# One attention and mixture-of-experts layer: rotary keys, latent query products and the second S5 turn set in another order

## The chip, the core and the metric

One core of a Trainium2 chip runs the whole program. The metric is device time in microseconds: 941.87 us, the median of 3 runs of the kernel before (941.67 to 942.17). In the profile PE is TensorE's matmul row and PEld its weight loads, DVE is VectorE, ACT ScalarE, POOL GpSimd, and SP the engine that issues most DMAs. Everything is computed in float32.

## What is computed

One layer for 512 latent tokens and 256 context tokens, width 1024. All tokens are normalised and modulated, and go through one input projection. Its columns feed three groups of heads:

```
z_lat = split_in_proj(modulate(rms_norm(x, norm_mix_g), sh_m, sc_m) @ w_in)    # u | q | k | v | cq | ckv | kr
z_ctx = split_in_proj(modulate(rms_norm(ctx, norm_mix_g), csh_m, csc_m) @ w_in)
s5  : h[t] = lam_bar * h[t-1] + b_bar @ u[t], forwards and backwards; y = Re(c_mat @ h) + d * u
      y = gelu(y);  y = y * sigmoid(y @ w_glu + b_glu)
diff: softmax(q0 k0') - lam * softmax(q1 k1'), times v; q and k of latent tokens are rotated
mla : q = rms_norm(cq) @ w_uq;  k_nope, v = rms_norm(ckv) @ w_ukv;  the 32 rotary columns kr are shared by all heads
x = x + g_m * (concat(s5, diff, mla) @ w_out)
x = rms_norm(x + g_f * moe(modulate(rms_norm(x, norm_ffn_g), sh_f, sc_f)))     # 32 experts, two per token
```

The modulation vectors (sh, sc, g) are silu(c) times a 1024 x 6144 matrix.

## The kernel before

Tokens stand in six tiles of 128: tiles 0 and 1 are context, 2 to 5 latent. Each engine has its program written out by hand, one list of steps per engine, and the steps meet at semaphores. An engine takes its own steps in the written order; nothing is planned at run time ahead of the experts. The list of TensorE (L941 to L1006) is the one that the change rewrites, with those of ScalarE (L1560 to L1611) and VectorE (L2174 to L2236).

The steps that matter here:

- `project(kind, t)` multiplies tile t with the columns of one kind: q, k, v are 512 wide, m (the latent columns cq, ckv, kr) 416 wide for a latent tile and 160 for context. Each is eight products over the model width. `project("uq", t)` is the latent query product, 2 products of 384 columns, from the turned cq of tile t. The result lands in one of four PSUM banks in turn; `z_bank` waits until the tile four places earlier in the list `ztiles` has been copied out (`z_free`).
- `evacuate(w)` on VectorE copies such a result out, rotated where it must be, into one of two buffers (QR). For v tiles `v_out` on ScalarE does it, or VectorE for v5 in the kernel before.
- `turn_tile(w)` transposes the copied tile on TensorE, into bank 4 or 5 by turns; `turn_out(w)` on ScalarE copies it to its place. The list `turns` numbers them: a turn waits for the turned tile two places earlier to be out.
- `turn_rope` transposes the rotary keys of all six tiles at once, into banks 4 and 5; ScalarE makes four copies of it (L1526), one per head.
- The S5 group: `s5_turn(d)` turns the input matrices of direction d, in four pieces c of four transposes, into banks 6 and 7, and ScalarE copies them out (`s5_evac_turned`, L1545). Pieces 2 and 3 wait for the copies of pieces 0 and 1. `s5_inputs(d, r)` multiplies them with u, VectorE's `s5_scan(d)` copies the results (L2059), runs the recurrence (L2083), and sets the flag `hh` (L2094) that `s5_outputs(d)` on TensorE waits for. The outputs of direction 1 also need taps (TPL) that POOL fetches after the last input product (L584 to L588). `s5_add` on VectorE (L2104) adds the outputs up.
- `mod_sum(g, r)` on VectorE adds up two of eight slices of a third of the modulation product from a 2 MB piece of w_mod; the piece's slot is free for the next load when it is done. `summed_rows` on TensorE sums them over partitions.
- `gated` is the S5 gate's product; `scores(u)` begins attention.

VectorE's list has m0, m1, m2, the scan of direction 1, m3, two modulation sums, `s5_add(1)`, m4, and so on. Around the scan it is the same in both kernels.

At the end, from about 440 us on, the experts run in blocks, and their weights (1 MB and 2 MB pieces) stream through the slots that the front has given back. Their loads are issued by SP, the first of them after all projected tiles are made and out, after attention, and after the output projection.

Of the kernel before, what the change touches and what calls it, by code (L numbers as in the profile page):

```python
# [75 lines left out]
def build(nc, a, out):  # L76
# [22 lines left out]
    with ctx:  # L99
# [219 lines left out]
        U_BANK = (0, 1, 6, 7, 0, 1)  # L319
        ztiles = [("u", n) for n in range(NU)]  # L320
        ztiles += [("q", t) for t in range(NCT, NT)] + [("k", t) for t in range(NT)] + [("m", t) for t in range(NT)]
        ztiles += [("v", t) for t in range(5)] + [("uq", 2), ("uq", 3), ("uq", 4), ("v", 5), ("g", 0), ("g", 1), ("uq", 5)]
        ztiles += [("kn", i) for i in range(4)] + [("nv", i) for i in range(3)]
        zi = {w: n for n, w in enumerate(ztiles)}
        turns = [w for w in ztiles if w[0] in ("q", "k", "m")] + [("uq", 2), ("uq", 3), ("kr", 0), ("uq", 4), ("uq", 5)]
        ti = {w: n for n, w in enumerate(turns)}
        ACT_TILES = (("nv", 0), ("nv", 1))

# [357 lines left out]
        def _(pe):  # L686
# [189 lines left out]
                                     start=(r == 0), stop=(r == 1))  # L876
                ins.then_inc(sem("kk"), 1)

            def s5_turn(d):
                pe.wait_ge(sem("pb"), d + 1)  # L880
                for c in range(4):
                    if c == 0:
                        pe.wait_ge(sem("ksb"), 2 * d + 1)
                    elif c >= 2:
                        pe.wait_ge(sem("pbt"), 4 * d + c - 1)
                    for j in range(4):
                        r, q = divmod(4 * c + j, NPAIR)
                        ins = tr(bank(6 + c % 2, P, j * P), PB[:, r, q].rearrange("p i n -> p (i n)"), ident)
                    ins.then_inc(sem("pb_t"), 1)
# [77 lines left out]
            project("m", 1)  # L967
            project("m", 2)
            turn_tile(("k", 5))
            s5_turn(1)  # L970
            turn_tile(("m", 0))
            s5_inputs(1, 0)
            turn_tile(("m", 1))
            s5_inputs(1, 1)
            project("m", 3)
            project("m", 4)
            project("m", 5)
            project("v", 0)
            turn_tile(("m", 2))
# [4 lines left out]
            pe.wait_ge(sem("yacc"), 4)  # L984
            project("v", 2)
            turn_tile(("m", 4))
            project("v", 3)
            turn_tile(("m", 5))
            summed_rows(1, 6, True)
            project("v", 4)  # L990
            project("uq", 2)
            project("uq", 3)
            project("uq", 4)
            project("v", 5)
            turn_tile(("uq", 2))
            turn_tile(("uq", 3))
            gated()
            turn_rope()
            project("uq", 5)
            turn_tile(("uq", 4))  # L1000
            summed_rows(2, 7, False)
            mod_rows(2, KD // 2 - 1, 7)
            turn_mod(1, 6)
            project_latent("kn", 0)
            project_latent("kn", 1)
            turn_tile(("uq", 5))  # L1006

            def scores(u):

# [407 lines left out]
        def _(act):  # L1417
# [121 lines left out]
                else:  # L1539
                    A(ksb[:, :, 0:7 * GRP], taps[:, :, 0:7 * GRP], ACT.Copy).then_inc(sem("ksb"), 1)  # L1540

            def s5_evac_turned(d):
                for c in range(4):
                    act.wait_ge(sem("pb_t"), 4 * d + c + 1)
                    A(PBT[:, c // 2, 4 * (c % 2):4 * (c % 2) + 4].rearrange("p q s -> p (q s)"), bank(6 + c % 2), ACT.Copy).then_inc(  # L1545
                        sem("pbt"), 1)
# [27 lines left out]
            squares_of_m(1)  # L1574
            squares_of_m(2)
            turn_out(("k", 5))
            s5_evac_turned(1)

            act.wait_ge(sem("k_out"), 16)
            turn_out(("m", 0))  # L1580
            turn_out(("m", 1))
            squares_of_m(3)
            squares_of_m(4)
            squares_of_m(5)
            def v_out(t):
                act.wait_ge(sem("z"), zi[("v", t)] + 1)
                act.wait_ge(sem("z_free"), zi[("v", t)])
                A(VV[:, t, :], bank(zi[("v", t)] % 4), ACT.Copy).then_inc(sem("z_free"), 1)

            turn_out(("m", 2))  # L1590
            turn_out(("m", 3))
            v_out(0)
# [1 line left out]
            turn_out(("m", 4))  # L1594
            v_out(2)
            turn_out(("m", 5))
            v_out(3)
            act.wait_ge(sem("gelu_in"), 1)
            A(yt1, yt1, ACT.Tanh, scale=math.sqrt(2.0 / math.pi)).then_inc(sem("tanh"), 1)
            v_out(4)  # L1600

            turn_out(("uq", 2))
            turn_out(("uq", 3))
            for mo in range(2):
                act.wait_ge(sem("z"), zi[("g", mo)] + 1)
                A(yt1[:, mo].rearrange("p j c -> p (j c)"), bank(zi[("g", mo)] % 4), ACT.Sigmoid,
                  bias=cols[:, R_BGLU + mo:R_BGLU + mo + 1]).then_inc(sem("s5_sig"), 1)
            turn_out(("kr", 0))
            mod_copy(1, 6)
            turn_out(("uq", 4))  # L1610
            turn_out(("uq", 5))  # L1611


# [168 lines left out]
        def _(dve):  # L1782
# [340 lines left out]
            def evacuate(w):  # L2123
                kind, t = w
                dve.wait_ge(sem("z"), zi[w] + 1)
                src = bank(zi[w] % 4)
                n = ti.get(w)
                if n is not None:
                    if n >= 2:
                        dve.wait_ge(sem("turned"), n - 1)  # L2130
                    dst = QR[:, n % 2, :]
                lt = t - NCT
                if kind in ("q", "k"):
                    if t >= NCT:
                        rope(dst.rearrange("p (h f) -> p h f", h=2 * DH), src.rearrange("p (h f) -> p h f", h=2 * DH),
                             2 * DH, DHD // 2, lt, 0)
                    else:
                        st(cp(dst, src))
                elif kind == "v":
                    st(cp(VV[:, t, :], src))  # L2140
                elif kind == "m":
                    dve.wait_ge(sem("m_ms"), t + 1)
                    if t >= NCT:
                        st(V.reciprocal(sml[:, 16 + t:17 + t], sml[:, 16 + t:17 + t]))
                    st(V.reciprocal(sml[:, 24 + t:25 + t], sml[:, 24 + t:25 + t]))
                    st.settle()
                    if t >= NCT:
                        st(ts(dst[:, 0:QRANK], src[:, 0:QRANK], sml[:, 16 + t:17 + t], None, ALU.mult))
                    st(ts(dst[:, QRANK:QRANK + KVRANK], src[:, QRANK:QRANK + KVRANK], sml[:, 24 + t:25 + t], None, ALU.mult))
                    kr = src[:, QRANK + KVRANK:QRANK + KVRANK + MR]  # L2150
                    if t >= NCT:
                        rope(KR[:, t:t + 1, :], kr.unsqueeze(1), 1, MR // 2, lt, 32)
                    else:
                        st(cp(KR[:, t, :], kr))
                elif kind == "uq":
                    s3 = src[:, 0:MH * MQ].rearrange("p (h f) -> p h f", h=MH)
                    d3 = dst[:, 0:MH * MQ].rearrange("p (h f) -> p h f", h=MH)
                    st(cp(d3[:, :, 0:MN], s3[:, :, 0:MN]))
                    rope(d3[:, :, MN:], s3[:, :, MN:], MH, MR // 2, lt, 32)
                elif kind == "kn":  # L2160
                    pr, half = divmod(t, 2)
                    t0, nt = (0, 512) if half == 0 else (512, TOK - 512)
                    for g in range(2):
                        st(cp(MKT[0:MN, 2 * pr + g, t0:t0 + nt], src[MN * g:MN * (g + 1), 0:nt]))
                else:
                    st(cp(MVV[:, 2 * t:2 * t + 2, :].rearrange("p t e -> p (t e)"), src))
                st.settle()
                if n is not None:
                    cp(sml[:, 506:507], epsb[:, :]).then_inc(sem("qr"), 1)
                if w == ("uq", 2):  # L2170
                    dve.wait_ge(sem("z_free"), zi[w])
                cp(sml[:, 507:508], epsb[:, :]).then_inc(sem("z_free"), 1)

# [20 lines left out]
            evacuate(("m", 4))  # L2194
            mod_sum(1, 2)
            evacuate(("m", 5))
            mod_sum(1, 3)
            dve.wait_ge(sem("y_in"), 32)
            for h in range(2):
                st(stt(YT[:, h], UT[:, h, :, NCC:], cols[:, R_SD + h:R_SD + h + 1], YT[:, h], ALU.mult, ALU.add))  # L2200
# [8 lines left out]
            st(ts(yt1, yt1, 0.5, 0.5, ALU.mult, ALU.add))  # L2209
            st.settle()  # L2210
            tt(YG, yt1, YT, ALU.mult).then_inc(sem("yg"), 1)
            mod_sum(2, 1)
            evacuate(("uq", 2))
            evacuate(("uq", 3))
            cp(sml[:, 511:512], epsb[:, :]).then_inc(sem("qr"), 1)
            mod_sum(2, 2)
            evacuate(("uq", 4))
            evacuate(("v", 5))
            dve.wait_ge(sem("yg"), 1)
            for mo in range(2):  # L2220
                dve.wait_ge(sem("s5_sig"), mo + 1)
                tt(mix[:, mo, :].rearrange("p (c j) -> p j c", j=CH), YG[:, mo], yt1[:, mo], ALU.mult).then_inc(
                    sem("s5_mix"), 1)
                cp(sml[:, 509 + mo:510 + mo], epsb[:, :]).then_inc(sem("z_free"), 1)
            evacuate(("uq", 5))
            mod_cols(1, (4, 4), 6, "modc")
            def maxima(u):
                dve.wait_ge(sem("scores"), u + 1)
# [523 lines left out]
```

## Time and profile before

| | |
|---|---|
| median of 3 runs | 941.87 us (941.67 to 942.17) |
| profiled execution | 944.54 us, its span 942.8 us |
| TensorE busy | 854.7 us, 91% of the span |
| VectorE, ScalarE busy | 451.1 us, 246.6 us |
| granted TensorE clock, mean | 0.975 |
| chain that ended last | PE 44%, issue 39%, POOL 5%, DVE 4%, DMA 3%, ACT 2% |

The chain is followed back from the last instruction to what released each step; "issue" is time in which an engine waited for nothing that the profile shows. A row of a timeline has the start in us, the busy time, the engine, the line and operation, what it writes and reads, how many instructions are merged, and in brackets the idle time before it and what ended that. Float32 products show as several records each, so 16 records of L854 are one tile of 8 products. The granted clock is 1.00 or 0.50 of full speed (2.4 or 1.2 GHz); a value between is a mean over the stretch.

### The profile page before, as it was taken

How to read it: one execution, taken by the hardware profiler on the slowest of the kernel's cores; microseconds unless marked ns; L12 is line 12 of the kernel's file. 1: busy time of each engine (PE TensorE's matmuls, PEld its weight loads, DVE VectorE, ACT ScalarE, POOL GpSimd, SP SyncE). 2: the span in 40 equal slices, each digit the busy share in tenths (PEclk: the TensorE clock that was granted, in tenths of full speed). 3: DMA queues.
4: the chain of work that ended last, by engine and by line, in shares of the span. 5: the costliest groups of instructions: out<-in, count | busy, mean ns of one | idle time of the engine just before them, and what ended most of it. 6: DMA issues, size and time to landing. Idle time of an engine off the chain costs nothing.

```text
span 942.8 us, 12686 instructions
## 1 busy us (share of the span) xinstructions
PE 854.7 (91%) x4395; PEld 431.5 (46%) x4395; DVE 451.1 (48%) x1112; ACT 246.6 (26%) x561; POOL 138.5 (15%) x376
## 2 busy tenths in 40 slices
PE   4999999999899999999999999999999976867786
PEld 1765546554445556446344444444444432333232
DVE  4596888978688674125652221312222321212127
ACT  4701023213467654022211120211111211111113
POOL 1411001020010010000012121212212222212110
PEclk9999999999999999999899999999999999788999
DMA  9961204586400391225989999999999999999985
GB/s 372 343 190 32 89 1 120 153 343 225 152 2 23 111 321 60 89 112 217 376 341 381 420 419 420 419 421 420 421 421 419 419 418 419 418 417 421 418 349 223
DMA packets 56373, 267.12 MB, mean 283 GB/s; under 512 B 10867, under 2 KB 17325, under 8 KB 29456
## 3 DMA queue, kind: packets, MB, share of 16 engines
q1 hardware_dynamic: 44416, 249.70, 65.9%
q0 software_dynamic: 11712, 16.86, 6.4%
q8 instruction: 23, 0.38, 0.2%
q14 instruction: 14, 0.11, 0.0%
q10 hardware_dynamic: 208, 0.06, 0.0%
HBM read 264.48 MB, written 25.17 MB: 307 GB/s over the span
## 4 chain that ended last, share of the span: by engine, by line
PE 44%; issue 39%; POOL 5%; DVE 4%; DMA 3%; ACT 2%; POOLq 1%; SPq 1%; DVEq 0%
PE PS L854 15%; PE PS L1089 6%; PE PS L1020 4%; POOL held L650 2%; PE PS L1027 2%; PE PS L1058 2%; DMA S5Z<-in_w_mod 2%; PE PS L778 2%; POOL BIG L659 2%; DMA BIG<-pair_d 1%; PE PS L1067 1%; PE PS L1218 1%; PE PS L924 1%; PE PS L1247 1%; PE PS L1319 1%
## 5 line engine op out<-in xcount | busy, mean ns | idle before, releaser
L854 PE MATMUL PS<-BIG 128*128 128x512 f32 (+2 forms) x352 | 139.6, 553 | 0.0
L854 PEld LDWEIGHTS PS<-BIG 128*128 128x128 f32 x352 | 64.2, 190 | 66.7 <-issue 66.1
L1322 PE MATMUL PS<-S5Z,QKV 128*128 128x512 f32 x192 | 83.4, 592 | 0.0
L1347 PE MATMUL PS<-BIG,GM 128*64 128x512 f32 x320 | 75.4, 614 | 4.0 <-DMA BIG<-in_moe_w 4.0
L650 POOL TENSOR_TENSOR held<-held 1x1 f32<-1x1 f32 x141 | 25.8, 183 | 302.2 <-PE PS L1295 178.4
L2670 DVE TENSOR_TENSOR QKV<-PS,QKV 64x512 f32<-64x512 f32 x48 | 33.0, 688 | 68.4 <-PE PS L1347 46.2
L1311 PE MATMUL PS<-BIG,QKV 128*32 128x256 f32 x768 | 49.5, 409 | 17.5 <-DMA BIG<-in_moe_w 17.5
L1319 PE MATMUL PS<-BIG,QKV 128*64 128x512 f32 x256 | 57.1, 596 | 3.9 <-DMA BIG<-in_moe_w 3.9
L1089 PE MATMUL PS<-BIG 128*128 128x512 f32 x128 | 57.0, 596 | 0.0
L1322 PEld LDWEIGHTS PS<-S5Z,QKV 128*128 128x128 f32 x192 | 36.1, 190 | 43.0 <-issue 43.0
L1720 ACT ACTIVATE QKV<-PS,fcp 128x128 f32<-128x128 f32 x120 | 45.1, 456 | 34.9 <-PE PS L1295 34.9
L2596 DVE TENSOR_SCALAR QKV<-PS,fcp 128x128 f32<-128x128 f32 x120 | 40.9, 403 | 21.6 <-PE PS L1295 21.6
L2229 DVE TENSOR_REDUCE sml<-PS 128x1 f32<-128x768 f32 x48 | 44.8, 952 | 12.8 <-PE PS L1020 12.6
L1295 PE MATMUL PS<-CST,BIG 128*128 128x128 f32 x240 | 37.2, 302 | 13.0 <-DMA BIG<-xh_d,gidx 13.0
L1731 ACT ACTIVATE wglu<-PS 128x256 f32<-128x256 f32 (+1 forms) x16 | 7.4, 464 | 156.6 <-PE PS L1322 80.1
L1295 PEld LDWEIGHTS PS<-CST,BIG 128*128 128x128 f32 x240 | 31.9, 196 | 31.7 <-DMA BIG<-xh_d,gidx 17.6
L1619 ACT ACTIVATE BIG<-PS,sml 128x768 f32<-128x768 f32 x48 | 43.1, 897 | 8.8 <-DVE sml L2229 8.4
L1352 PE MATMUL PS<-S5Z,GM 128*128 128x512 f32 x96 | 43.9, 612 | 0.0
L2602 DVE TENSOR_TENSOR GM<-wglu,PS 64x256 f32<-64x256 f32 x15 | 6.4, 425 | 74.8 <-ACT wglu L1728 74.8
L1311 PEld LDWEIGHTS PS<-BIG,QKV 128*32 128x32 f32 x768 | 24.6, 116 | 37.4 <-DMA BIG<-in_moe_w 20.7
L1347 PEld LDWEIGHTS PS<-BIG,GM 128*64 128x64 f32 x320 | 22.0, 141 | 42.9 <-issue 41.4
L2606 DVE TENSOR_TENSOR GM<-wglu,PS 128x512 f32<-128x512 f32 x6 | 4.1, 688 | 78.4 <-ACT wglu L1731 78.4
(576 smaller groups left out, 1239.3 us busy)
## 6 DMA issues: line engine op xcount, KB each, us to landing
BIG<-in_moe_w SPq DMA_DIRECT2D x84, 1024.0 KB, 22.5
BIG<-in_moe_w SPq DMA_DIRECT2D x21, 2048.0 KB, 25.7
S5Z<-in_moe_w SPq DMA_DIRECT2D x40, 1024.0 KB, 20.7
BIG<-in_w_mod SPq DMA_DIRECT2D x11, 2048.0 KB, 7.7
S5Z<-in_moe_w SPq DMA_DIRECT2D x10, 2048.0 KB, 24.3
BIG<-in_w_in SPq DMA_DIRECT2D x3, 2048.0 KB, 18.7
QKV<-in_x SPq DMA_DIRECT2D x8, 512.0 KB, 8.8
BIG<-in_w_out SPq DMA_DIRECT2D x2, 2048.0 KB, 10.9
```

Of the source, the lines that this page charges most:

```text
L650: pool.tensor_tensor(held[:, cell:cell + 1], held[:, 0:1], held[:, 0:1], ALU.add)
L854: ins = mm(dst[:, c0:width], hT[:, k, tok], wslot(n, width)[:, k, c0:width], start=(k == 0), stop=(k == KD - 1))
L1089: ins = mm(bank(op_bank(i)), mix[:, k, t * P:(t + 1) * P], wslot(n)[:, k, :], start=(k == 0), stop=(k == KD - 1))
L1295: ins = tr(bank(k // 4, P, (k % 4) * P), hg.rearrange("p (q k) -> p k q", k=KD)[:, k, :], ident)
L1311: ins = mm(PS[32 * n:32 * n + 32, 1024:1280], few, w13(side)[:, w, k, 256 * m:256 * m + 256], start=(k == 0), stop=(k == KD - 1))
L1319: ins = mm(PS[r, 1024:1536].rearrange("p (m h) -> p m h", m=2), few, w13(side)[:, :, k, 256 * m:256 * m + 256], start=(k == 0), stop=(k == ...
L1322: ins = mm(bank(2 + m), hgT[:, k, :], w13(side)[:, m, k, :], start=(k == 0), stop=(k == KD - 1))
L1347: ins = mm(PS[64 * n:64 * n + 64, 2560:3072], hidT[:, k % 2, 64 * (k // 2):64 * (k // 2) + 64], w2s(side)[:, k, 512 * n:512 * (n + 1)], st ...
L1352: ins = mm(bank(5 + n), hidT[:, k, :], w2s(side)[:, k, 512 * n:512 * (n + 1)], start=(k == 0), stop=(k == 3))
L1619: A(pbuf[:, 2 * (b % 2) + m, :], unit_row(u), ACT.Exp, bias=sml[:, 64 + u:65 + u], accum_out=sml[:, 160 + u:161 + u]).then_inc(sem("probs" ...
L1720: ins = A(hgT[:, k, :], bank(0, P, k * P), ACT.Identity, scale=fcp[:, 0, k:k + 1], bias=fcp[:, 1, k:k + 1])
L2229: V.tensor_reduce(sml[:, 64 + u:65 + u], unit_row(u), AX.X, ALU.max, negate=True).then_inc(sem("nmax"), 1)
```

## The change

TensorE's list is reordered in two places, and the lists of ScalarE and VectorE follow.

1. The turn of S5's direction 1 is cut in two halves. Pieces 0 and 1 come behind k5's turn as before. Then m0's turn and the product of latent row tile m3 stand ahead of pieces 2 and 3, and m1's turn and the product of m4 stand ahead of both input groups. Before, both input groups came ahead of m3.
2. The rotary keys are turned behind m5's turn and the product uq3, ahead of the summed rows. Before, they came behind the gate's product. The latent query products uq2 to uq5, before three in a row between v4 and v5 and one behind the rotary turn, are spread between the v tiles. v5 goes to ScalarE. VectorE copies uq2 and uq3 ahead of the GELU's input, uq4 and uq5 behind it. No instruction on data is added or left out.

The diff, cut to its core:

```diff
         ztiles = [("u", n) for n in range(NU)]
         ztiles += [("q", t) for t in range(NCT, NT)] + [("k", t) for t in range(NT)] + [("m", t) for t in range(NT)]
-        ztiles += [("v", t) for t in range(5)] + [("uq", 2), ("uq", 3), ("uq", 4), ("v", 5), ("g", 0), ("g", 1), ("uq", 5)]
+        ztiles += [("v", 0), ("v", 1), ("v", 2), ("uq", 2), ("uq", 3), ("v", 3), ("uq", 4), ("v", 4), ("uq", 5), ("v", 5)]
+        ztiles += [("g", 0), ("g", 1)]
         ztiles += [("kn", i) for i in range(4)] + [("nv", i) for i in range(3)]
         zi = {w: n for n, w in enumerate(ztiles)}
-        turns = [w for w in ztiles if w[0] in ("q", "k", "m")] + [("uq", 2), ("uq", 3), ("kr", 0), ("uq", 4), ("uq", 5)]
+        turns = [w for w in ztiles if w[0] in ("q", "k", "m")] + [("kr", 0)] + [("uq", t) for t in range(NCT, NT)]
         ti = {w: n for n, w in enumerate(turns)}
...
@@ -967,13 +968,14 @@
             project("m", 1)
             project("m", 2)
             turn_tile(("k", 5))
-            s5_turn(1)
+            s5_turn(1, (0, 1))
             turn_tile(("m", 0))
+            project("m", 3)
+            s5_turn(1, (2, 3))
+            turn_tile(("m", 1))
+            project("m", 4)
             s5_inputs(1, 0)
-            turn_tile(("m", 1))
             s5_inputs(1, 1)
-            project("m", 3)
-            project("m", 4)
             project("m", 5)
             project("v", 0)
             turn_tile(("m", 2))
@@ -984,26 +986,26 @@
             pe.wait_ge(sem("yacc"), 4)
             project("v", 2)
             turn_tile(("m", 4))
+            project("uq", 2)
+            turn_tile(("m", 5))
+            project("uq", 3)
+            turn_rope()
+            summed_rows(1, 6, True)
             project("v", 3)
-            turn_tile(("m", 5))
-            summed_rows(1, 6, True)
+            turn_tile(("uq", 2))
+            project("uq", 4)
             project("v", 4)
-            project("uq", 2)
-            project("uq", 3)
-            project("uq", 4)
+            turn_tile(("uq", 3))
+            project("uq", 5)
             project("v", 5)
-            turn_tile(("uq", 2))
-            turn_tile(("uq", 3))
+            turn_tile(("uq", 4))
             gated()
-            turn_rope()
-            project("uq", 5)
-            turn_tile(("uq", 4))
+            turn_tile(("uq", 5))
             summed_rows(2, 7, False)
             mod_rows(2, KD // 2 - 1, 7)
             turn_mod(1, 6)
             project_latent("kn", 0)
             project_latent("kn", 1)
-            turn_tile(("uq", 5))
...
@@ -1574,19 +1576,20 @@
             squares_of_m(1)
             squares_of_m(2)
             turn_out(("k", 5))
-            s5_evac_turned(1)
-
-            act.wait_ge(sem("k_out"), 16)
-            turn_out(("m", 0))
-            turn_out(("m", 1))
-            squares_of_m(3)
-            squares_of_m(4)
-            squares_of_m(5)
+            s5_evac_turned(1, (0, 1))
+
...
+            act.wait_ge(sem("k_out"), 16)
+            turn_out(("m", 0))
+            s5_evac_turned(1, (2, 3))
+            squares_of_m(3)
+            turn_out(("m", 1))
+            squares_of_m(4)
+            squares_of_m(5)
             turn_out(("m", 2))
             turn_out(("m", 3))
             v_out(0)
@@ -1594,20 +1597,20 @@
             turn_out(("m", 4))
             v_out(2)
             turn_out(("m", 5))
-            v_out(3)
+            turn_out(("kr", 0))
             act.wait_ge(sem("gelu_in"), 1)
             A(yt1, yt1, ACT.Tanh, scale=math.sqrt(2.0 / math.pi)).then_inc(sem("tanh"), 1)
+            v_out(3)
+            turn_out(("uq", 2))
+            mod_copy(1, 6)
             v_out(4)
-
-            turn_out(("uq", 2))
             turn_out(("uq", 3))
+            v_out(5)
+            turn_out(("uq", 4))
...
-            turn_out(("kr", 0))
-            mod_copy(1, 6)
-            turn_out(("uq", 4))
             turn_out(("uq", 5))
...
@@ -2194,7 +2197,10 @@
             evacuate(("m", 4))
             mod_sum(1, 2)
             evacuate(("m", 5))
+            cp(sml[:, 511:512], epsb[:, :]).then_inc(sem("qr"), 1)
             mod_sum(1, 3)
+            evacuate(("uq", 2))
+            evacuate(("uq", 3))
...
             tt(YG, yt1, YT, ALU.mult).then_inc(sem("yg"), 1)
+            evacuate(("uq", 4))
             mod_sum(2, 1)
-            evacuate(("uq", 2))
-            evacuate(("uq", 3))
-            cp(sml[:, 511:512], epsb[:, :]).then_inc(sem("qr"), 1)
+            evacuate(("uq", 5))
             mod_sum(2, 2)
-            evacuate(("uq", 4))
-            evacuate(("v", 5))
```

TensorE around the second S5 turn, before. L888 are the turns of the input matrices, L815 the turns of m0 and m1, L903 the input products, L854 with 128x416 the latent row tiles, with 128x512 v0, L917 the first of the outputs:

```order
L888 MATMUL PS<-CST,BIG 128x128 x16
L815 MATMUL PS<-CST,S5Z 128x128
L903 MATMUL PS<-S5Z 64x96 x16
L815 MATMUL PS<-CST,S5Z 128x128
L903 MATMUL PS<-S5Z 64x96 x16
L854 MATMUL PS<-BIG 128x416 x24
L854 MATMUL PS<-BIG 128x512 x8
L815 MATMUL PS<-CST,S5Z 128x128 x3
L917 MATMUL PS<-S5Z 128x64 x16
```

and in the changed kernel, where all lines behind the lists stand one number higher:

```order
L889 MATMUL PS<-CST,BIG 128x128 x8
L816 MATMUL PS<-CST,S5Z 128x128
L855 MATMUL PS<-BIG 128x416 x8
L889 MATMUL PS<-CST,BIG 128x128 x8
L816 MATMUL PS<-CST,S5Z 128x128
L855 MATMUL PS<-BIG 128x416 x8
L904 MATMUL PS<-S5Z 64x96 x32
L855 MATMUL PS<-BIG 128x416 x8
L855 MATMUL PS<-BIG 128x512 x8
L816 MATMUL PS<-CST,S5Z 128x128 x3
L918 MATMUL PS<-S5Z 128x64 x16
```

One latent tile has moved ahead of the second half turn, one more ahead of the input products, which stand together now.

TensorE around the rotary keys, before. L716 are the summed rows, L860 the latent query products, L818 their turns, L937 the gate, L827 the turn of the rotary keys:

```order
L716 MATMUL PS<-BIG,CST 32x512 x4
L854 MATMUL PS<-BIG 128x512 x8
L860 MATMUL PS<-wuq,S5Z 128x384 x6
L854 MATMUL PS<-BIG 128x512 x8
L818 MATMUL PS<-CST,S5Z 96x128 x8
L937 MATMUL PS<-S5Z,wglu 128x512 x4
L827 MATMUL PS<-CST,S5Z 32x128 x6
L860 MATMUL PS<-wuq,S5Z 128x384 x2
L818 MATMUL PS<-CST,S5Z 96x128 x4
```

and in the changed kernel:

```order
L861 MATMUL PS<-wuq,S5Z 128x384 x2
L816 MATMUL PS<-CST,S5Z 128x128 x3
L861 MATMUL PS<-wuq,S5Z 128x384 x2
L828 MATMUL PS<-CST,S5Z 32x128 x6
L717 MATMUL PS<-BIG,CST 32x512 x4
L855 MATMUL PS<-BIG 128x512 x8
L819 MATMUL PS<-CST,S5Z 96x128 x4
L861 MATMUL PS<-wuq,S5Z 128x384 x2
L855 MATMUL PS<-BIG 128x512 x8
L819 MATMUL PS<-CST,S5Z 96x128 x4
L861 MATMUL PS<-wuq,S5Z 128x384 x2
L855 MATMUL PS<-BIG 128x512 x8
```

The rotary turn has moved from the place behind the gate to the one ahead of the summed rows, and between each latent query product and its turn there is a v tile, or the summed rows and a v tile.

## Rows read from the trace of the kernel before

**Rows 1.** Windows: busy us (instructions) of each engine, granted clock, DMA share, GB/s.

```profile
182.00:249.00 67.00, 64.50 (x281) 33.61 (x281) 51.85 (x96) 17.69 (x32) 5.88 (x11) 0.97 0.74 279
467.00:915.00 448.00, 395.65 (x2272) 177.89 (x2268) 116.87 (x281) 71.69 (x200) 94.64 (x260) 0.96 1.00 410
```

**Rows 2.** Timeline of TensorE, second S5 turn; columns as told above.

```profile
152.70 1.04 PE L888 MATMUL PS<-CST,BIG 128*128 128x128 f32 x8
154.87 1.14 PE L888 MATMUL PS<-CST,BIG 128*128 128x128 f32 x8 [1.13 <-ACT S5Z L1545]
...
156.70 1.54 PE L903 MATMUL PS<-S5Z 128*64 128x96 f32 x32 [0.58 <-ACT S5Z L1545]
...
158.76 1.54 PE L903 MATMUL PS<-S5Z 128*64 128x96 f32 x32 [0.26 <-DVE BIG L2059]
160.23 23.04 PE L854 MATMUL PS<-BIG 128*128 128x416 f32 x62
```

**Rows 3.** Timeline of TensorE, end of the projections.

```profile
237.07 1.46 PE L860 MATMUL PS<-wuq,S5Z 128*128 128x384 f32 x4
240.35 0.61 PE L818 MATMUL PS<-CST,S5Z 128*96 128x128 f32 x4 [1.82 <-ACT S5Z L1526]
240.90 1.87 PE L716 MATMUL PS<-BIG,CST 128*32 128x512 f32 x8
242.52 2.85 PE L707 MATMUL PS<-BIG,silu_c 128*32 128x512 f32 x16
...
248.37 1.55 PE L1020 MATMUL PS<-QKV 64*128 64x512 f32 x4 [0.68 <-ACT S5Z L1522]
```

**Rows 4.** Windows: stretches at either clock, and idle ones.

```profile
241.00:244.30 3.30, 3.30 (x20) 0.78 (x24) 0.00 (x0) 0.59 (x1) 0.00 (x0) 0.50 1.07 390
449.50:455.80 6.30, 5.10 (x13) 1.25 (x12) 3.66 (x22) 0.00 (x0) 0.00 (x0) 0.50 1.02 427
782.00:788.00 6.00, 2.96 (x40) 1.91 (x40) 0.42 (x1) 0.38 (x1) 0.08 (x1) 1.00 1.01 417
858.00:862.00 4.00, 0.19 (x4) 0.00 (x0) 0.00 (x0) 0.00 (x0) 0.87 (x1) 1.00 1.02 419
862.50:865.50 3.00, 2.99 (x29) 1.38 (x32) 0.00 (x0) 0.00 (x0) 0.00 (x0) 0.50 1.04 421
```

**Rows 5.** Timeline of VectorE: scan, first sum, S5 sum, GELU product.

```profile
158.07 1.01 DVE L2059 COPY BIG<-PS 128x384 f32<-128x384 f32 x2
...
179.03 0.15 DVE L2094 COPY sml<-epsb 128x1 f32<-128x1 f32 x1
...
181.00 1.29 DVE L1894 TENSOR_SCALAR BIG<-BIG,silu_c 128x2048 f32<-128x2048 f32 x1
...
191.79 1.29 DVE L2104 TENSOR_TENSOR S5Z<-PS,S5Z 128x512 f32<-128x512 f32 x2 [2.32 <-PE PS L924]
...
218.98 1.23 DVE L2211 TENSOR_TENSOR S5Z<-S5Z 128x1024 f32<-128x1024 f32 x1
```

**Rows 6.** Timeline of TensorE: S5 outputs and v1.

```profile
183.96 0.49 PE L815 MATMUL PS<-CST,S5Z 128*128 128x128 f32 x3
184.29 3.68 PE L917 MATMUL PS<-S5Z 128*128 128x64 f32 x32
...
191.62 7.13 PE L854 MATMUL PS<-BIG 128*128 128x512 f32 x16
198.59 0.49 PE L815 MATMUL PS<-CST,S5Z 128*128 128x128 f32 x3
```

**Rows 7.** Groups by line, VectorE, 182 to 250 us: busy us, mean ns.

```profile
L1898 DVE SCALAR_TENSOR_TENSOR BIG<-BIG,silu_c 128x2048 f32<-128x2048 f32 x7 | 16.5, 2352 | 0.2
```

**Rows 8.** The page, DMA issues: count, KB each, us to landing.

```profile
BIG<-in_w_mod SPq DMA_DIRECT2D x11, 2048.0 KB, 7.7
```

**Rows 9.** Timeline of TensorE: modulation rows and summed rows, full clock.

```profile
21.29 1.92 PE L707 MATMUL PS<-BIG,silu_c 128*32 128x512 f32 x16 [1.79 <-DMA BIG<-in_w_mod]
...
213.41 1.06 PE L716 MATMUL PS<-BIG,CST 128*32 128x512 f32 x8
```

More of the change, by code:

```diff
@@ L877, in s5_kernel, with s5_turn @@
                 ins.then_inc(sem("kk"), 1)
-            def s5_turn(d):
+            def s5_turn(d, parts=range(4)):
                 pe.wait_ge(sem("pb"), d + 1)
-                for c in range(4):
+                for c in parts:
                     if c == 0:
@@ L1540, in s5_evac_kernel, with s5_evac_turned @@
                     A(ksb[:, :, 0:7 * GRP], taps[:, :, 0:7 * GRP], ACT.Copy).then_inc(sem("ksb"), 1)
-            def s5_evac_turned(d):
-                for c in range(4):
+            def s5_evac_turned(d, parts=range(4)):
+                for c in parts:
                     act.wait_ge(sem("pb_t"), 4 * d + c + 1)
@@ L2169, in evacuate @@
                     cp(sml[:, 506:507], epsb[:, :]).then_inc(sem("qr"), 1)
-                if w == ("uq", 2):
+                if ztiles[zi[w] - 1][0] == "v":
                     dve.wait_ge(sem("z_free"), zi[w])
@@ L2223, in _ @@
                     sem("s5_mix"), 1)
+                if mo == 0:
+                    dve.wait_ge(sem("z_free"), zi[("g", 0)])
                 cp(sml[:, 509 + mo:510 + mo], epsb[:, :]).then_inc(sem("z_free"), 1)
-            evacuate(("uq", 5))
             mod_cols(1, (4, 4), 6, "modc")
```

## The prediction

> **What bounds the kernel now.** I read the stretches first [rows 1]. From 467 to 915 us the DMA engines are busy the whole time (share 1.00, 410 GB/s): the expert weights stream, and TensorE follows them. Their first buffers are released by TensorE's own progress, so what starts later in front ends later behind. In the stretch of the change, from 182 to 249 us, TensorE is busy 64.50 of 67 us while DMA runs at 0.74: this part is bound by TensorE and by the few places where it stands still. So the timeline of TensorE comes next, and for each gap the row of the engine that ends it. There are two places. In the S5 turn of the backward direction [rows 2] TensorE waits 1.13 us for ScalarE's copy (L1545), 0.58 for the next, and 0.26 for VectorE's copy of the S5 inputs. At the end of the projections [rows 3] it waits 1.82 us for the rotary-key copies (L1526) and then 0.68 us for the last query copy (L1522); behind the 1.82 the granted clock is 0.50 from 241.0 to 244.3 us [rows 4], the lower of the two levels, 1.2 GHz.
>
> **What must be on time between these two.** VectorE's scan (L2059 to L2094) reads the four S5 input products. Its first copy starts at 158.07 us and the flag for the outputs is set at 179.03 [rows 5]. TensorE comes to the outputs (L917, L924) at 184.29 [rows 6], 5.1 us after the flag. That is all the slack there is, and VectorE's order around the scan is not changed.
>
> **Part one: the S5 turn in halves.** Removed: 1.13 + 0.58 + 0.26 = 1.97 us of named waits, and with the drained array around them about 2.3. Before, TensorE takes 184.29 - 152.70 = 31.6 us from the first half turn to the outputs; without these it takes 29.3 and arrives at 182.0.
> Added ahead of the input products: two latent row tiles of eight products. The stretch from 160.23 to 183.96 is three of these and one v tile; a v tile takes 198.59 - 191.62 = 6.97 us [rows 2, 6], so one latent tile takes (23.73 - 6.97) / 3 = 5.6 us. The new row of work is: 8 turns 0.9 us (half of what the rows show for 16, hand-over included), one tile turn 0.1, m3 5.6, 8 turns 0.9, one tile turn 0.1, m4 5.6, both input groups 1.5 + 1.5 and a hand-over of 0.1. From 152.70 this ends at 169.0. Before, the inputs ended at 160.30. The scan therefore ends 8.7 us later, at 187.8 with the hand-over. VectorE stands idle meanwhile, since its next work is the scan.
> What is late next: TensorE, there at 182.0, has the outputs at the head of its row and waits for the flag until 187.8, 5.8 us. Behind it are v1, m3's turn and everything after. So 2.3 us are taken away and 5.8 put in: the outputs start at 187.8 instead of 184.29, +3.5. The other wait of the outputs, the taps that POOL fetches after the last input product, moves by the same 8.7 us, to about 180, and is covered. ScalarE's copies have both new tiles as cover.
>
> **VectorE after the scan.** It now runs without a break from 187.8: m3's copy 1.9 (179.14 to 181.00 before), four modulation sums (a pair of slices is 1.29 + 2.35 us for the first [rows 5] and 2 x 2.35 for the others [rows 7]), 3.7 + 4.8 + 4.8 + 4.8, the S5 sum 1.3, m4 and m5 1.9 each. This ends at 212.9. Before, it waited 2.3 us at the S5 sum for TensorE [rows 5]; now it is VectorE that comes last there, at 198.1. TensorE needs the S5 sum after v1, at 187.8 + 7.3 + 7.0 = 202.1: covered by 2.7 us. It needs the fourth modulation sum for the summed rows after v2, two latent query products and the rotary turn, at about 213.4: covered by 0.5 us only, which is the thinnest cover in this change. The weights of the sums land 7.7 us after issue [rows 8]; each is issued when the sum two before is done, and the next but one is always over 7.7 us away, or within 0.3 of it. Sums for the third group end near 239.5, TensorE wants them at 243: covered. The S5 sum is 6.4 us late and the gate's input with it: before finished at 220.2 [rows 5], now near 227. The gate is wanted at 239.
>
> **Part two: rotary keys and latent query products.** The rotary keys are turned right behind m5. ScalarE's four copies of them lie beside v3, 7 us of TensorE. Each latent query product (1.3 us) now has a v tile between itself and its turn, so VectorE's copy of it is over in time. Both named waits go, 1.82 + 0.68 us. With them goes the low clock: at full clock eight products of the summed rows take 1.06 us and sixteen of the modulation rows 1.92 [rows 9]; at 0.50 they took 1.87 and 2.85 [rows 3]. That is 1.7 us. Sum of part two: -4.2 us. The matmul and copy counts are the same, nothing is added. The keys' copies need the S5 results out of the way (y_out), 208 us by the shift above, and are wanted at 213.6. The last w_mod load is issued near 233.5 and is used at 244, the w_out loads near 239 are used at 374: both are covered.
>
> **The clock behind the new gap.** No row of before has a gap of 5.8 us. The nearest are mixed [rows 4]: behind 858 to 862, almost idle, the clock is 0.50 from 862.5 to 865.5; after the gap of 1.82 us it is 0.50 for 3.3 us; and 449.5 to 455.8 shows 6.3 us of it; but from 782 to 788, idle for the first half, it is 1.00 throughout. So from one side the price is nothing. From the other it is 6.3 us at half speed, 3.2 us. I take 3.4 us at half speed, 1.7 us, as behind the 1.82 us gap: some of the low stretch may pass while TensorE is still waiting.
> The Trainium skill ("TensorE: Matmul & The Clock Gate", section "Why this matters for your kernels") warns against idle gaps between bursts of matmuls, because they bring the engine back to half clock. By that rule the fall is certain, and the sum is the one below; without it the sum is the rival with the clock kept. The trace agrees at 858 us, and not at 782.
>
> **The sum.** +3.5 (outputs later) - 4.2 (part two) + 1.7 (clock) = +1.0 us at the first scores, 249.4 instead of 248.37. Behind the scores the order of work is the same and waits hang on each other, so the shift is carried to the end one to one; the DMA stretch keeps its length. The profiled execution took 944.54 us, 1.74 of it outside its span of 942.8, and is 2.67 over the median of the runs; it would become 945.5, and the median 941.87 becomes 942.9.
>
> **The rivals.** A change under 0.2% (1.9 us) can't be told from none here.
> 1. The clock is kept through the new gap. For it: 782 us. Against it: 862.5, 241, 449.5. The time is 941.87 - 0.7 = 941.2.
> 2. The low clock is long: 6.3 us or more after the restart, as in the stretch from 449.5. Place: the outputs and v1. Price: 3.2 us instead of 1.7. It decides for slower once more than 5.2 us of low clock fall behind the restart (0.7 + 1.9 = 2.6, times two). Late outputs also use up the 0.5 us of cover at the summed rows, though TensorE's own delay widens it again. Against it: 3.3 us at 241. Time: 941.87 - 0.7 + 3.2 = 944.4.
> 3. The scan isn't late: VectorE has its inputs soon enough, or the 5.1 us of slack are larger than read, and only the gains are left: -2.3 - 4.2 = -6.5 us, 935.4. For it: all removed waits are real. Against it: the order puts two tiles of 5.6 us ahead of the inputs, and the slack is read from single rows [rows 5, 6].
> 4. The change doesn't do what it says in the tail: the rotary turn waits for m5's copies, of which it is only one turn and one product behind, and TensorE stands there instead. ScalarE's order has v2, m5 and the keys in a row, so 1 us may come back: 943.9.
>
> **How the numbers follow.** Forecast 0.52, rival one 0.12, rival two 0.20, rival three 0.12, rival four 0.04. The forecast's own spread is 942.0 to 944.0, so a few hundredths of it are slower; rivals two and four are mostly slower, rival one is no change, rival three is faster, and 0.01 of the others. Faster 0.13, no change 0.62, slower 0.25. The range leaves out rival three and reaches from rival one less 0.6 us for what the trace of one execution can't tell, 940.6, to rival two plus 0.4, 944.8.
>
> **What would show it.** TensorE waits 5 to 6.5 us ahead of L918 (L917 of before), ended by VectorE, and starts it at 187 to 188.5 us. The gaps at 153 to 159 us are gone, VectorE is idle from about 156 to 166. The granted clock is 0.50 for some us behind the wait, and is 1.00 from 236 to 248. No wait on the rotary keys' copies. The first scores start at 249.4 +- 1. I am wrong if the outputs start by 184, if the clock stays at 1.00, or if a new wait stands at the summed rows or ahead of the scores.

## The result, and the profile after

The changed kernel takes 951.19 us (median of 4, 950.46 to 952.04), the kernel before 942.02 us in the same comparison: ratio 1.0092, interval 1.0079 to 1.0105. It is slower by 9.2 us. The forecast was 942.9, no change. One disturbed execution of 2221 us, in the run with ten filling products below, is left out of its median and interval.

TensorE's timeline of the changed kernel answers to [rows 2, 3, 6]. L889 are the turns of the S5 input matrices, L904 the input products, L918 and L925 the outputs, L828 the rotary turn:

```profile
153.65 1.04 PE L889 MATMUL PS<-CST,BIG 128*128 128x128 f32 x8
...
154.63 5.75 PE L855 MATMUL PS<-BIG 128*128 128x416 f32 x16
160.22 1.04 PE L889 MATMUL PS<-CST,BIG 128*128 128x128 f32 x8
...
161.20 5.75 PE L855 MATMUL PS<-BIG 128*128 128x416 f32 x16
166.89 3.17 PE L904 MATMUL PS<-S5Z 128*64 128x96 f32 x64
...
182.55 0.49 PE L816 MATMUL PS<-CST,S5Z 128*128 128x128 f32 x3
189.01 7.09 PE L918 MATMUL PS<-S5Z 128*128 128x64 f32 x32 [5.96 <-DVE sml L2097]
196.02 7.09 PE L925 MATMUL PS<-BIG,S5Z 64*128 64x64 f32 x64
203.05 8.61 PE L855 MATMUL PS<-BIG 128*128 128x512 f32 x16
...
221.93 0.82 PE L828 MATMUL PS<-CST,S5Z 128*32 128x128 f32 x6
...
251.71 0.60 PE L819 MATMUL PS<-CST,S5Z 128*96 128x128 f32 x4
...
256.83 1.55 PE L1022 MATMUL PS<-QKV 64*128 64x512 f32 x4
```

The three waits of [rows 2] are gone, as are the two of [rows 3], and one has come: 5.96 us ahead of the outputs, ended by VectorE's flag (now L2097). Behind it L918 takes 7.0 us until the next row starts, instead of 3.6, L925 7.0 instead of 3.7, and v1 8.4 instead of 7.0.

VectorE, against [rows 5]: the first copy of the input products waits 10.95 us, the flag comes at 188.80 instead of 179.03, and the S5 sum now waits 4.01 us for the outputs instead of 2.32.

```profile
167.81 1.22 DVE L2062 COPY BIG<-PS 128x384 f32<-128x384 f32 x2 [10.95 <-PE PS L904]
...
188.80 0.15 DVE L2097 COPY sml<-epsb 128x1 f32<-128x1 f32 x1
...
203.22 1.29 DVE L2107 TENSOR_TENSOR S5Z<-PS,S5Z 128x512 f32<-128x512 f32 x2 [4.01 <-PE PS L925]
```

The windows of the same stretch, columns as in [rows 1], show why the rows behind the gap are long. The third number from the end is the granted clock:

```profile
183.00:189.00 6.00, 0.04 (x1) 0.00 (x0) 5.83 (x10) 0.88 (x3) 0.00 (x0) 0.71 0.46 193
189.00:196.00 7.00, 6.99 (x32) 6.90 (x32) 6.76 (x15) 0.00 (x0) 0.00 (x0) 0.50 0.11 18
196.00:203.00 7.00, 7.00 (x65) 6.91 (x64) 3.17 (x2) 0.00 (x0) 0.00 (x0) 0.50 0.97 391
203.00:206.00 3.00, 3.00 (x6) 1.41 (x5) 2.71 (x12) 0.00 (x0) 1.20 (x3) 0.50 1.02 427
206.00:211.50 5.50, 5.50 (x14) 2.34 (x14) 4.87 (x5) 0.00 (x0) 3.30 (x7) 1.00 0.56 108
```

From the end of the gap to 206 us TensorE is busy all the time, at 0.50 (1.2 GHz). The clock falls inside the gap, at 185.5 us, and comes back 20.5 us later. [Rows 4] have stretches of 3.0 to 6.3 us. PEld, the second busy time, shows the weight loads: they take 13.8 of the outputs' 14.0 us, and 1.41 of 3.00 in v1.

### The profile page after: what moved, and what is told of

It is laid out like the page before. It is cut to its first block, busy times and chain, and to the rows that moved or that the text cites. A ratio compares the mean times of both kernels' runs of the same rounds, so it can differ in the third digit from the quotient of the medians.

```text
span 950.0 us, 12686 instructions
## 1 busy us (share of the span) xinstructions
PE 866.0 (91%) x4395; PEld 440.2 (46%) x4395; DVE 450.4 (47%) x1110; ACT 246.5 (26%) x562; POOL 138.2 (15%) x376
## 4 chain that ended last, share of the span: by engine, by line
PE 43%; issue 39%; DVE 6%; POOL 5%; DMA 3%; ACT 1%; POOLq 1%; SPq 1%; DVEq 0%
PE PS L855 13%; PE PS L1091 6%; PE PS L1022 4%; POOL held L651 2%; PE PS L1029 2%; PE PS L1060 2%; DMA BIG<-in_w_mod 2%; PE PS L779 2%; POOL BIG L660 2%; PE PS L1069 1%; PE PS L925 1%; DMA BIG<-pair_d 1%; PE PS L1220 1%; DVE sml L2233 1%; PE PS L1249 1%
## 5 line engine op out<-in xcount | busy, mean ns | idle before, releaser
L2233 DVE TENSOR_REDUCE sml<-PS 128x1 f32<-128x768 f32 x48 | 44.8, 952 | 12.5 <-PE PS L1022 12.2
L1297 PE MATMUL PS<-CST,BIG 128*128 128x128 f32 x240 | 39.1, 313 | 11.7 <-DMA BIG<-xh_d,gidx 11.7
## 6 DMA issues: line engine op xcount, KB each, us to landing
S5Z<-in_moe_w SPq DMA_DIRECT2D x40, 1024.0 KB, 21.5
```

The lines of the kernel that those rows point to most:

```text
L1297: ins = tr(bank(k // 4, P, (k % 4) * P), hg.rearrange("p (q k) -> p k q", k=KD)[:, k, :], ident)
L2233: V.tensor_reduce(sml[:, 64 + u:65 + u], unit_row(u), AX.X, ALU.max, negate=True).then_inc(sem("nmax"), 1)
```

## The experiments

Three comparisons, each with runs of the kernel before on the same chip; ratios are against those.

### One part at a time

The tail alone, with the second S5 turn as before (TensorE's part; ScalarE's list goes with it):

```diff
-            s5_turn(1, (0, 1))
-            turn_tile(("m", 0))
-            project("m", 3)
-            s5_turn(1, (2, 3))
-            turn_tile(("m", 1))
-            project("m", 4)
-            s5_inputs(1, 0)
-            s5_inputs(1, 1)
+            s5_turn(1)
+            turn_tile(("m", 0))
+            s5_inputs(1, 0)
+            turn_tile(("m", 1))
+            s5_inputs(1, 1)
+            project("m", 3)
+            project("m", 4)
```

> The changed kernel with the second S5 turn put back as before: only the rotary keys and the latent query products stay moved. Sum of the prediction for this part alone: 1.82 + 0.68 us of waits and 1.7 us of low clock go, 4.2 us, so 937.8. The outputs start near 184.3 at a clock of 1.00. Rival (the moved tail is worth nothing, or costs): 942 or more, with a new wait between 205 and 248 us.

Measured: 939.33 us against 942.42, ratio 0.9965 (0.9952 to 0.9978). Its TensorE:

```profile
153.19 1.04 PE L889 MATMUL PS<-CST,BIG 128*128 128x128 f32 x8
...
184.78 3.68 PE L918 MATMUL PS<-S5Z 128*128 128x64 f32 x32
...
239.30 0.60 PE L819 MATMUL PS<-CST,S5Z 128*96 128x128 f32 x4
...
244.42 1.55 PE L1021 MATMUL PS<-QKV 64*128 64x512 f32 x4
```

No wait stands ahead of L819 (L818 before). From the outputs to the first scores it takes 244.42 - 184.78 = 59.6 us, before 64.1 [rows 3, 6]: 4.4 us are gained, 4.2 were forecast. 3.1 of them are left in the median. In the profiled execution the clock falls once at 257 us, behind the scores' own waits, and attention's rows take 1.3 us longer there; that this is the whole difference is not shown.

The S5 turn alone, the reverse of the diff above in the kernel before:

> The kernel before with only the second S5 turn cut in halves. If the loss is the late outputs (+3.5 us) and the low clock behind the gap (8.2 us in the changed kernel), this is slower than the changed kernel by what its tail gained: about 942.0 + 3.5 + 8.2 = 953.7, with the low clock from about 185 to 205 us. Rival (the long low clock comes from the two parts together): low clock for some 3 us only and 947.

Measured: 954.42 us, ratio 1.0125 (1.0108 to 1.0142), 12.0 us slower than the kernel before; 11.7 had been expected (953.7 against 942.0). Gap and slow outputs are the changed kernel's:

```profile
188.53 7.09 PE L917 MATMUL PS<-S5Z 128*128 128x64 f32 x32 [5.96 <-DVE sml L2096]
195.55 7.09 PE L924 MATMUL PS<-BIG,S5Z 64*128 64x64 f32 x64
202.57 8.70 PE L854 MATMUL PS<-BIG 128*128 128x512 f32 x16
...
252.87 0.61 PE L818 MATMUL PS<-CST,S5Z 128*96 128x128 f32 x4 [1.82 <-ACT S5Z L1527]
```

So the halves lose 12.0 us and the tail gains 3.1 in the medians. Together that is 8.9, and the changed kernel is 9.2 us slower: the two add up.

### The gap and the clock

Filling TensorE's wait ahead of the outputs with products of constants, results not used, in the changed kernel; n is 8, 10 or 4:

```diff
             turn_tile(("m", 2))
+            pe.wait_ge(sem("bu_out"), 8)
+            warm(n, 6)                  # n products of 384 columns
             s5_outputs(1)
```

> The changed kernel with eight products of constants (128 columns by 384, results not used) put into TensorE's wait ahead of the S5 outputs: the outputs still start when VectorE's flag comes, near 188 us. If the clock is what costs, it stays 1.00, the outputs take 7.3 us instead of 14.0, and the time is 942.0 - 0.7 = 941.3, or up to 943. Rival (the loss has another cause): 949 to 951.

Measured: 943.92 us, ratio 1.0023 (1.0007 to 1.0039). Nine of 12 executions took 942.47 to 945.10 us, three 948.01 to 950.38. The profiled one was of the three (949.52):

```profile
181.88 5.33 PE L739 MATMUL PS<-CST 128*128 128x384 f32 x16
188.01 4.61 PE L918 MATMUL PS<-S5Z 128*128 128x64 f32 x32 [0.81 <-DVE sml L2099]
192.55 7.09 PE L925 MATMUL PS<-BIG,S5Z 64*128 64x64 f32 x64
199.57 9.52 PE L855 MATMUL PS<-BIG 128*128 128x512 f32 x16
```

With eight products a wait of 0.81 us was left over, and in this execution the clock fell at 190.8 us, among the outputs, and came back at 204.4. In nine of 12 the time is the one that the theory asks for or up to 2 us more; that the clock stayed at 1.00 in them is inferred from their times, as none of them has a trace. The other three suggest that even this small gap can be enough.

> As the kernel with eight filling products, with ten, 6.6 us of them: TensorE comes to the S5 outputs behind VectorE's flag and doesn't wait at all. With eight, a wait of 0.81 us was left, and 3 of 12 executions took 948.0 to 950.4 us, the others 942.5 to 945.1; in the profiled one (949.52) the clock fell at 190.5 us. Theory (the outputs can't hold the clock once any gap leads into them): all executions within 942.5 to 945. Rival (the outputs let the clock fall by themselves): again some near 949.

Measured: 942.75 us, ratio 1.0016 (1.0005 to 1.0027); the 11 executions lie between 940.90 and 945.73, none near 949. The outputs take 3.6 and 3.7 us, though they start as late behind the first half turn as in the changed kernel (35.7 us, there 35.4):

```profile
181.91 6.62 PE L739 MATMUL PS<-CST 128*128 128x384 f32 x20
188.36 3.68 PE L918 MATMUL PS<-S5Z 128*128 128x64 f32 x32
191.97 3.79 PE L925 MATMUL PS<-BIG,S5Z 64*128 64x64 f32 x64
195.69 7.13 PE L855 MATMUL PS<-BIG 128*128 128x512 f32 x16
```

Some 8 us of the changed kernel's time hang on whether TensorE works or waits in these 6 us. Neither this trace nor the other ten times show the outputs letting the clock fall by themselves. Three of 12 against none of 11 could still be chance; that the last 0.81 us make this difference is likely and not shown.

> The same with four filling products, 2.7 us: a gap of about 3.3 us ahead of the outputs instead of 6. If the price depends on what follows the gap and not on its length, the clock is low until v1 as in the changed kernel, and the time is 950 to 951, hardly less than with the whole gap. If the price goes with the length, it is half: 946 to 947.

Measured: 951.10 us, ratio 1.0100 (1.0084 to 1.0116), as much as with the whole gap. The wait is 3.38 us; the clock is low from 189.1 to 206.2:

```profile
187.97 6.07 PE L918 MATMUL PS<-S5Z 128*128 128x64 f32 x32 [3.38 <-DVE sml L2099]
193.97 7.09 PE L925 MATMUL PS<-BIG,S5Z 64*128 64x64 f32 x64
200.99 9.70 PE L855 MATMUL PS<-BIG 128*128 128x512 f32 x16
```

Half the gap costs as much as the whole. What the price goes with is shown by wide products behind the wait:

```diff
             turn_tile(("m", 2))
+            pe.wait_ge(sem("bu_out"), 8)
+            pe.wait_ge(sem("hh"), 2)
+            warm(5, 6)
             s5_outputs(1)
```

> The changed kernel with five wide products of constants behind the wait and ahead of the S5 outputs; the gap itself stays. Theory (the low clock lasts because the small output products of 64 columns don't release it, wide ones do): half clock for about 3.3 us of wide products, then 1.00; the burst adds 5 us, the outputs and v1 give back 8.2: 948. Rival (the length of the gap alone sets how long the clock is low, some 20 us whatever follows): 951.2 + 6.6 = 957.8, outputs again 14 us.

Measured: 949.03 us, ratio 1.0071 (1.0054 to 1.0088): 4.8 us of added work, and still some 2 us faster than the changed kernel (all four executions lie below 949.4, all of the changed kernel above 950.4).

```profile
188.79 4.96 PE L739 MATMUL PS<-CST 128*128 128x384 f32 x10 [6.06 <-DVE sml L2100]
193.58 3.68 PE L918 MATMUL PS<-S5Z 128*128 128x64 f32 x32
197.19 3.79 PE L925 MATMUL PS<-BIG,S5Z 64*128 64x64 f32 x64
200.91 7.13 PE L855 MATMUL PS<-BIG 128*128 128x512 f32 x16
```

```profile
185.50:188.50 3.00, 0.00 (x0) 0.00 (x0) 2.90 (x5) 0.00 (x0) 0.00 (x0) 0.50 0.03 11
188.80:191.80 3.00, 3.00 (x5) 1.79 (x6) 2.79 (x13) 0.00 (x0) 0.00 (x0) 0.50 0.00 0
192.50:200.50 8.00, 8.00 (x96) 7.42 (x94) 6.33 (x3) 0.00 (x0) 0.00 (x0) 1.00 0.67 228
```

The gap is whole (6.06 us) and the clock falls as before, at 185 us. The 384-column products run for 3 us at 0.50, then it is 1.00, and the outputs take 7.3 us. In the changed kernel the same outputs ran 14 us at 0.50 and it came back only among the 512-column products of v1.

Narrowness is not the only thing that sets the outputs apart. Beside the wide products, in the 3 us at 0.50, the weight loads take 1.79 us; beside the outputs they take nearly all the time. Which of the two keeps the clock low, the few columns or the time that goes into weight loads, no run here separates.

### Orders without the gap

The input products ahead of m4, all else as in the changed kernel:

```diff
             turn_tile(("m", 1))
-            project("m", 4)
             s5_inputs(1, 0)
             s5_inputs(1, 1)
+            project("m", 4)
```

> The changed kernel with the S5 input products ahead of latent row tile m4 instead of behind it; m3 stays between the half turns. The inputs end 5.6 us earlier, near 163.5, the scan's flag comes near 182.5, when TensorE arrives. Theory (all depends on TensorE not standing still ahead of the outputs): no gap or under 1 us, clock 1.00, and 942.0 - 1.5 - 4.2 = 936.3. Rival (the split turn costs of itself): 942 or more.

Measured: 937.75 us (937.39 to 938.42), ratio 0.9951 (0.9937 to 0.9965), the fastest of all, 4.2 us under the kernel before where 5.7 had been expected.

```profile
161.89 3.17 PE L904 MATMUL PS<-S5Z 128*64 128x96 f32 x64 [0.63 <-ACT S5Z L1547]
...
184.01 3.79 PE L918 MATMUL PS<-S5Z 128*128 128x64 f32 x32 [0.38 <-DVE sml L2097]
...
243.76 1.55 PE L1022 MATMUL PS<-QKV 64*128 64x512 f32 x4
```

The gap ahead of the outputs is 0.38 us, a new one of 0.63 stands ahead of the inputs. It was run again beside the third group:

> The kernel with the input products ahead of m4 once more, on the same chip as the one without any gap, for comparison: 937.8 as before (4.2 us under the kernel before).

938.19 us (937.48 to 940.23), ratio 0.9965 (0.9951 to 0.9979). Of the five and six executions none is near 949. The second time 3.1 us are gained, as much as by the tail alone (ratio 0.9965 too). Its first scores start at 242.85 us, 1.6 us ahead of the tail alone, 1.0 of it behind the first half turn; that the split turn gains anything of this in the whole time is not shown.

v1 ahead of the outputs, and the wait for the S5 sum behind v2:

```diff
             turn_tile(("m", 2))
-            s5_outputs(1)
             project("v", 1)
+            s5_outputs(1)
             turn_tile(("m", 3))
-            pe.wait_ge(sem("yacc"), 4)
             project("v", 2)
+            pe.wait_ge(sem("yacc"), 4)
```

> The changed kernel with v1's product ahead of the S5 outputs, and the wait for the S5 sum behind v2. v1 needs m3's bank, which VectorE frees behind the scan, near 190.7, so the gap grows from 6 to about 7.8 us, but a wide product follows it. Theory (wide products release the clock): low clock for some 3 us of v1, outputs in 7.3 us, 946.5. Rival (only the gap's length matters): clock low for 20 us, v1 13 us and outputs slow, 955 or more.

Measured: 953.58 us, ratio 1.0114 (1.0099 to 1.0130). Half of the expectation held: the clock came back among v1's products and the outputs took 7.3 us. But v2's bank is m4's, which VectorE frees behind the S5 sum, which waits for the outputs that now stand right ahead of v2: 2.81 us more, and a second low clock (v2 9.5 us).

```profile
189.87 9.44 PE L855 MATMUL PS<-BIG 128*128 128x512 f32 x16 [7.87 <-DVE sml L2175]
199.15 3.68 PE L918 MATMUL PS<-S5Z 128*128 128x64 f32 x32
202.76 3.79 PE L925 MATMUL PS<-BIG,S5Z 64*128 64x64 f32 x64
...
209.84 9.70 PE L855 MATMUL PS<-BIG 128*128 128x512 f32 x16 [2.81 <-DVE sml L2175]
```

With m3 copied ahead of the scan as well (VectorE: `evacuate(("m", 3))` ahead of `s5_scan(1)`):

> As the kernel with v1 ahead of the S5 outputs, and VectorE copies m3 ahead of the scan, where it stands idle from 157 to 168 us. v1's bank is free in time, TensorE works on v1 while the scan runs, and no gap is left: clock 1.00, both sets of waits gone, 942.0 - 2.3 - 4.2 = 935.5. Rival: VectorE, late by 8.7 us, holds TensorE later, at the S5 sum or the summed rows; 938 to 942.

Measured: 943.30 us, ratio 1.0009 (1.0000 to 1.0018). The first gap is gone, the second stays and is the rival's, 2.95 us, with v2 at 9.9 us:

```profile
182.93 7.03 PE L855 MATMUL PS<-BIG 128*128 128x512 f32 x16
189.80 3.68 PE L918 MATMUL PS<-S5Z 128*128 128x64 f32 x32
...
200.62 10.08 PE L855 MATMUL PS<-BIG 128*128 128x512 f32 x16 [2.95 <-DVE sml L2175]
```

With m4 copied right behind the scan, m5 behind the S5 sum, and the summed rows behind v3:

> The kernel with v1 ahead of the outputs and m3 copied ahead of the scan, which lost 2.95 us and a low clock of 7 us at v2, because m4's bank was freed behind the S5 sum. Here VectorE copies m4 right behind the scan and m5 right behind the S5 sum, and the summed rows come behind v3. Theory: no gap over 0.5 us between 153 and 250 us, clock 1.00 there, all 6.5 us of gain: 935.5. Rival: VectorE's order can't be met and another wait of 2 us or more appears: 938 to 942.

Measured: 940.61 us (937.98 to 949.09), ratio 0.9996 (0.9976 to 1.0015): no change, with a wide spread. Up to 237 us there is no gap over 0.1 us, but then VectorE's last modulation sum (L1901) holds the summed rows of the third group for 3.27 us, and the clock is low from 240.8 to 244.3 us:

```profile
197.15 7.03 PE L855 MATMUL PS<-BIG 128*128 128x512 f32 x16
...
241.04 1.94 PE L717 MATMUL PS<-BIG,CST 128*32 128x512 f32 x8 [3.27 <-DVE BIG L1901]
```

The expectation of 935.5 missed; its rival was right. One execution took 949.09 us. The trace is of another one and has no gap ahead of the outputs; what slowed this one is open.

## Why the prediction was wrong

By its own steps:

- **The S5 turn.** Forecast: 2.3 us of waits gone, TensorE 29.3 us from the first half turn to the outputs, a wait of 5.8 us. Measured: 182.88 - 153.65 = 29.2 us and 5.96 us. The outputs start 3.8 us late against 3.5, once the 0.95 us are taken off that this execution had lost earlier (153.65 against 152.70, with a low clock from 21.5 to 25.5 us that [rows 9] don't have). Right.
- **VectorE after the scan.** The thin cover at the summed rows was never tested, because TensorE was later than thought. Nothing waited there. At the S5 sum the forecast had VectorE come last, at 198.1; it waited 4.01 us for the slow outputs instead.
- **The tail.** Forecast 4.2 us; from the outputs to the first scores the changed kernel takes 67.8 us against 64.1, and 8.2 of it are the slow outputs and v1, so 4.5 are gained. Right at the first scores, and by itself in the tail alone, 4.4.
- **The clock behind the new gap.** Forecast 1.7 us, bound 3.2 from above. Measured: 14.0 - 7.3 = 6.7 us in the outputs and 8.44 - 6.97 = 1.5 in v1, 8.2 together. This is the step that failed: a term of the sum, mis-sized by 6.5 us. I took the length of the low stretch from [rows 4], as if it belonged to the gap, and its longest as a bound. Here it went with the work behind it: the low stretches at 241 and 449.5 us ran products of 512 columns, and the S5 outputs are 48 products of 64 columns (96 records), behind which the clock was still at 0.50. That they ran at 1.00 when it was there [rows 6] hid it. The row that spoke for a kept clock was also read too short: the trace of before shows 1.00 through a wait of 3.08 us at 782, but behind the next one, 2.08 us, it is 0.50 from 790.8. The kernel with its gap filled, with half a gap, and with wide products behind it, show this from three sides. The Trainium skill ("TensorE: Matmul & The Clock Gate", section "Part 1: The HAM clock gate") says that activity releases the throttle; here TensorE was busy 7.00 of 7.00 us without it, so being busy in the profile's sense was not enough.
- **The sum.** 0.95 + 3.8 + 8.2 - 4.5 = 8.5 us at the first scores (256.83 against 248.37), 9.2 in the medians. With 1.7 in the third place, and without the 0.95, it would have been the forecast. Rival two had the right mechanism, place and side, but its price was less than half of the true one, so the range ended 6.4 us below the result. Neither it nor the forecast asked whether the work behind the gap sets how long the clock stays low, and the length of the gap, which the nearest rows were chosen by, did not decide: 3.4 us of it cost what 6 did.
- **One to one to the end.** Roughly. From the first scores of the traces to the medians, 8.5 us became 9.2 in the changed kernel, 12.5 became 12.0 with the turn alone, and 7.5 became 9.8 with half the gap. Gains shrank: 4.0 became 3.1 in the tail alone, and 5.5 became 3.1 with the input products ahead of m4, the second time. Why is open.

## What to carry to other kernels

Price a new wait of TensorE by the work that stands behind it. The low clock cost 8.2 us in the S5 outputs and v1, and 1.6 to 3.1 us where 384- or 512-column products stood behind the wait, though these waits were 2.8 to 7.9 us long. If a wait leads into many small products, a wide tile in front of them shortens the low stretch, but look which bank the tile needs: here the first try brought a second wait. If nothing can be put there, leave the old, shorter waits where they are: taking 2.3 us of waits away here cost 12. When a producer's step moves back behind two tiles, its consumer's slack must be larger than the two; one tile (5.6 us against 5.1 of slack) left a wait of 0.4 us and was 3.1 to 4.2 us faster together with the tail, which alone gains 3.1; two tiles lost.

## What the runs showed of the hardware

- In one and the same order, with a gap of 0.81 us ahead of the S5 outputs, nine executions took 942.5 to 945.1 us and three 948.0 to 950.4. In the only one with a trace, of the three, the clock fell 2.8 us into the outputs. Behind gaps of 3.4 and 6 us it was low in each profiled execution.
- Forty-eight float32 products of 64 columns (96 records), at 0.50, ran for 14 us, TensorE busy throughout, and the clock did not return. Behind them, and in the three runs in which 512- or 384-column products stood first behind a gap (wide products first, v1 first, m3 early), it returned 3 to 6 us after the wide ones began.
- The same low clock cost 1.6 us in five 384-column products (4.8 us instead of 3.2), 2.4 and 2.7 us in v1 and v2 with v1 ahead of the outputs, and 3.1 us in v2 with m3 copied early.
- At 1.00 the same 48 products ran 7.3 us and the clock held (the kernel before, the tail alone, with the gap closed, and behind a gap of 0.4 us with the input products ahead of m4).
